# Rates of the DeltaNet heads: weights stationary in four column groups, then a sum by token

## The chip, the cores and the metric

One NeuronCore of a Trainium2 chip runs the whole program. The metric is the device time of one execution in microseconds (us); the median over several executions stands for a kernel.

## The reference, cut to what matters

The kernel is one inference step of a decoder trunk of two layers for 256 prompt tokens and 32 sample tokens (8 sequences of 4), 288 in all, with 1024 channels. Each layer projects its normed input `h` onto about 3000 columns. Eight of these columns are the rates of the four DeltaNet heads: a write strength `beta` and a decay `g` per head and token. Everything is float32.

```python
proj = h @ w_in[layer]
qkv_in, z, b_raw, a_raw, glu_u, glu_g = jnp.split(proj, [o1, o2, o3, o4, o5], axis=-1)
beta = jax.nn.sigmoid(b_raw)                               # (tokens, 4)
g = -jnp.exp(a_log) * jax.nn.softplus(a_raw + dt_bias)     # (tokens, 4)
o_a, s = gated_delta_rule(q, k, v, g, beta, s0)            # chunks of tokens, state carried
```

`b_raw` and `a_raw` together are `h` (288 x 1024) times an array of 1024 x 8. That product is what the change touches. Layer 1 ends in a router that multiplies `h` with another array of 1024 x 8.

## The kernel before

Channels lie on partitions: a tensor of 1024 channels is eight tiles (k = 0 to 7) of 128 partitions by T = 288 tokens. The normed input is kept three times: `hf` in float32 and `h_hi`, `h_lo`, its rounded part and the rest. Weights arrive as units of 1 MB in six buffers `raw`, in one order that is written out by hand (`SEQUENCE`). The queue of SyncE (SP) issues the load of unit u once unit u - 6 is used up. Some units are split by ScalarE (ACT, `split_hi`) and VectorE (DVE, `split_lo`, tile `wlo`) into `whi` and `wlo` before TensorE (PE) uses them; one such tile is 24 matmuls (L1669 to L1671). A tile from an unsplit unit is eight matmuls (L2014), each of two records in the trace, as are all plain float32 matmuls here.

The stage around the change is `project_in`, once per layer, twelve steps i = 0 to 11 of two tiles each. Steps 0 to 3 make the Conformer half, 4 to 9 the q, k and v tiles, 10 and 11 the output gate. Every engine has its own program with its own loop over i, and semaphores tie them together:

- PE: both tiles of a step (`project_tile`), then `token_rates` after i = 2, `decay_sums` after i = 5, then `ada_columns` and `ada_pair`. The last two make the modulation vectors: `ada_pair` (L1680) holds the conditioning vectors `cstat` stationary, 32 columns per k, writes tile k to partitions 32k to 32k + 31, and streams 512 weight columns; `ada_columns` (L1690) sums the four groups with a constant `comb` while it turns rows into columns. In layer 0 the pairs run after i = 1 to 8 with the columns one step later, in layer 1 the pairs from i = 2. A pair uses two units, and their buffers are what the next loads wait for.
- ACT: row copies (L681) for the pairs, the sigmoid of the Conformer gate (L761) at i = 0 to 3, `token_gates` at i = 4 (beta and half of the softplus), the exponentials of the decays at i = 6, copies of the q, k, v tiles, and `split_hi` two steps ahead.
- DVE: `fill` runs a fixed number of Conformer taps per step (`TAPS_IN`, L1108), `copy_rates` and `decay_steps` at i = 3, `decay_rates` at i = 4, `copy_decays` at i = 6, `conv_pair` from i = 5 (L1128), `modulation` at i = 10 (L1058, L1061), and `split_lo` two steps ahead.

`token_rates` multiplies with the tokens stationary: for three blocks of tokens (128, 128 and 32) and eight k, `hf` is the stationary operand and the eight weight columns stream (L1991). That is 24 matmuls per layer into 24 columns of PSUM bank 4, one group of eight per block. `decay_sums` later writes to columns 32 to 55 of the same bank. PE's `sums_qk` (L1805), after i = 9, waits for the `modulation` of i = 10.

The router of layer 1 (L2099) is already written the other way, with its weights stationary in four column groups, a copy, and a sum by token (L2114).

Of the kernel before, what the change touches and what calls it, by code (L numbers as in the profile page):

```python
# [34 lines left out]
P = 128  # L35
D = 1024
KD = D // P
# [140 lines left out]
for _l in range(DEPTH):  # L178
# [9 lines left out]
CCOL, NCONST = columns(  # L188
    [("ones", P), ("comb", NC_), ("eps6", 1), ("eps5", 1), ("epsq", 1), ("one", 1), ("ident", P), ("tri", P), ("after", P), ("m1l", P), ("m1t", P)]
    + [(f"mt{s}", P) for s in LEVELS] + [("outA", P), ("outQ", P), ("outAS", TS), ("outQS", TS)]  # L190
    + [("before", P), ("iota", P), ("triS", P), ("afterS", P), ("seqp", NB),
       ("ipart", 1), ("valid", 1),
       ("rank", 3 * NE), ("eye8", NE + 1)])

# [3 lines left out]
def constants():  # L198

    c = np.zeros((P, NCONST), np.float32)  # L200

    def put(name, a):
        lo, _ = CCOL[name]
        c[:a.shape[0], lo:lo + a.shape[1]] = a

    i, j = np.arange(P)[:, None], np.arange(P)[None, :]
    put("ones", np.ones((P, P)))
    put("ident", i == j)
    put("tri", i <= j)
    put("after", i > j)  # L210
    low = lambda s: (i // (2 * s) == j // (2 * s)) & (i % (2 * s) >= s) & (j % (2 * s) < s)
    put("m1l", low(1))
    put("m1t", low(1).T)
    for s in LEVELS:
        put(f"mt{s}", low(s).T)
    put("outA", np.where(i > j, -FAR, FAR))
    put("outQ", np.where(i <= j, FAR, -FAR))
    put("before", i < j)
    put("iota", np.broadcast_to(j, (P, P)))
    same = (i // TD == j // TD) & (i < TS) & (j < TS)  # L220
    put("triS", same & (i <= j))
    put("afterS", same & (i > j))
    put("outAS", np.where(same & (i > j), -FAR, FAR)[:TS, :TS])
    put("outQS", np.where(same & (i <= j), FAR, -FAR)[:TS, :TS])
    put("seqp", np.arange(P)[:, None] % TS // TD == np.arange(NB)[None, :])
    put("comb", np.concatenate([np.eye(P // 4, NC_)] * 4) * (i % (P // 4) < NC_))
    put("eps6", np.full((P, 1), 1e-6))
    put("eps5", np.full((P, 1), 1e-5))
    put("epsq", np.full((P, 1), P * 1e-6))
    put("one", np.ones((P, 1)))  # L230
    put("ipart", i)
    put("valid", i < TS)
    put("rank", np.broadcast_to(NE - np.tile(np.arange(NE), 3)[None, :], (P, 3 * NE)))
    put("eye8", np.eye(NE))
    return c
# [19 lines left out]
def program(nc, units, x_in, c_in, par_in, const_in, gdn_in, qst_in, cst_in,  # L255
            y_out, gdnp_out, gdns_out, qst_out, cst_out):
    ctx = ExitStack()
    with ctx:
# [165 lines left out]
        router_ready, parts_done, parts_copied = sem("router_ready"), sem("parts_done"), sem("parts_copied")  # L424
        moe_added = sem("moe_added")
        conv_first, conv_step = sem("conv_first"), sem("conv_step")
        qsq_ready, qss_ready, qrs_ready, qn_ready = sem("qsq_ready"), sem("qss_ready"), sem("qrs_ready"), sem("qn_ready")
        cmean_done, cent_ready, csq_ready, css_ready = sem("cmean_done"), sem("cent_ready"), sem("csq_ready"), sem("css_ready")
        crs_ready, cn_ready, cy_ready = sem("crs_ready"), sem("cn_ready"), sem("cy_ready")
# [226 lines left out]
        def _(act):  # L656
# [66 lines left out]
            def project_in(l):  # L723
                round_h(2 * l)
                for i in range(LEAD):
                    if i in SPLIT_IN[l]:
                        split_hi(in_split(l, i))
                for i in range(N_IN):
                    if i - 1 in ADA_BEHIND[l]:
                        row_copy(*ADA_BEHIND[l][i - 1], 1, 5 + (i - 1) % 2)  # L730
                    if i == 4:
                        token_gates(l)
                    if i == 6:
                        act.wait_ge(cum_ready, l + 1)
                        act.activation(eg, ps[:, 4, 32:56], ACT.Exp).then_inc(eg_ready, 1)
                    if I_QKV + 2 <= i < I_QKV + 2 + N_CONV - 1:
                        silu_tile(l, 2 * (i - I_QKV - 2))
                        silu_tile(l, 2 * (i - I_QKV - 2) + 1)
# [294 lines left out]
        def _(dve):  # L1033
# [105 lines left out]
            def project_in(l):  # L1139
# [4 lines left out]
                for i in range(N_IN):  # L1144
# [4 lines left out]
                        modulation(l, 1)  # L1149
                    if I_QKV < i <= I_QKV + N_CONV:  # L1150
                        conv_pair(l, i - I_QKV - 1)
                    if i == 3:
                        copy_rates(l)
                        decay_steps(l)
                    fill(l, TAPS_IN[l][i])
                    if i in SUMS_IN:
                        sample_taps(l, SUMS_IN[i])
                    if i in CONF_UNITS:
# [24 lines left out]
            def copy_rates(l):  # L1183

                step(dve.memset(ab, 0.0))
                dve.wait_ge(ab_done, l + 1)
                dve.tensor_copy(ab[:, 0:16], ps[:, 4, 0:16])
                dve.tensor_copy(ab[0:TS, 16:24], ps[0:TS, 4, 16:24]).then_inc(ab_copied, 1)

            def decay_steps(l):  # L1190

# [16 lines left out]
            def copy_decays(l):  # L1208

                dve.wait_ge(eg_ready, l + 1)  # L1210
                dve.wait_ge(beta_ready, l + 1)
                dve.tensor_copy(gcs, ps[:, 4, 32:44])
                dve.tensor_tensor(bEG, beta, eg[:, 0:12], ALU.mult).then_inc(beg_ready, 1)
                dve.wait_ge(beg_ready, l + 1)

# [221 lines left out]
            dve.wait_ge(par_loaded, 16)  # L1437
            modulation(0, 0)
            norm(0)
            dve.wait_ge(masks_loaded, 16)  # L1440
            project_in(0)
            mixer(0)
# [214 lines left out]
        def _(pe):  # L1657
# [326 lines left out]
            def token_rates(l):  # L1984

                pe.wait_ge(hf_ready, 4 * l + 2)
                a, _ = PCOL[f"wab{l}"]
                for b in range(3):
                    n = TS if b == 2 else P
                    for k in range(KD):  # L1990
                        last = mm(ps[0:n, 4, 8 * b:8 * b + 8], hf3[:, k, b * P:b * P + n], par[:, a + 8 * k:a + 8 * k + 8],  # L1991
                                  start=(k == 0), stop=(k == KD - 1))
                last.then_inc(ab_done, 1)

            def project_tile(l, i, s):
# [21 lines left out]
            def project_in(l):  # L2017

                for i in range(N_IN):
                    project_tile(l, i, 0)  # L2020
                    if i == N_IN - 1:
                        for b in range(2):
                            transpose_a(l, b, b, P)
                    project_tile(l, i, 1)
                    if i == 0:
                        pe.wait_ge(mod_ready, 1 + 2 * l)
                        pe.wait_ge(rstd_ready, 1 + 2 * l)
                    if i == 2:
                        token_rates(l)
                    if i == 5:  # L2030
                        decay_sums(l)
                    if i - 1 in ADA_BEHIND[l]:
                        ada_columns(*ADA_BEHIND[l][i - 1], 1)
                    if i in ADA_BEHIND[l]:
                        ada_pair(*ADA_BEHIND[l][i], 5 + i % 2)
                    if i == I_QKV + 5:
                        sums_qk(l)
                    if i == N_IN - 2:
                        pe.wait_ge(qrs_ready, 5 * l + 4)
                        for b in range(2):  # L2040
                            row_decays(l, b, b, P)
                        pe.wait_ge(qn_ready, 5 * l + 4)
                        for b in range(2):
                            pe.wait_ge(bank_free[b], uses_at[l][b])
                            block_products(l, b, b, P)

            def decay_sums(l):

                pe.wait_ge(g_ready, l + 1)
                for mask, maskS, c in (("tri", "triS", 32), ("after", "afterS", 44)):  # L2050

                    mm(ps[:, 4, c:c + 8], cc(mask), gg[:, 0:8], start=True, stop=True)
                    last = mm(ps[:, 4, c + 8:c + 12], cc(maskS), gg[:, 8:12], start=True, stop=True)
# [299 lines left out]
```

## Time and profile before

| | us |
|---|---|
| median of 3 runs | 1787.5 |
| lowest, highest | 1779.77, 1791.13 |
| span of the profiled execution | 1782.5 |
| PE busy in it | 1735.4 (97%) |
| DVE busy | 1370.1 (77%) |
| ACT busy | 1034.4 (58%) |

The profile is of one execution, whose span goes from the first to the last instruction. All durations below are from it. Busy shares are means over very different stages, so what an edit is worth has to be read in its own stage. The two projection stages stand at about 36 to 162 us (layer 0) and 514 to 633 us (layer 1).

### The profile page before, as it was taken

The numbers are of one execution on the slowest core, as the hardware profiler recorded it, in microseconds if no ns is written. First come the engines' busy times: TensorE is split into PE (matmuls) and PEld (weight loads), VectorE is DVE, ScalarE is ACT, GpSimd is POOL, SyncE is SP. The second block draws the span as 40 slices with busy tenths as digits, with TensorE's granted clock in tenths as the row PEclk, the third lists the DMA queues.
The fourth block names the chain that finished last, engine by engine and source line by source line (L and its number), as shares of the span: only waits on it lengthen the run. The fifth ranks groups of instructions, "written<-read, shape, count | busy, mean of one in ns | idle before, by whom it ended". The sixth has DMA issues, their size and how long they took to land.

```text
span 1782.5 us, 25547 instructions
## 1 busy us (share of the span) xinstructions
PE 1735.4 (97%) x9512; PEld 1452.5 (81%) x9512; DVE 1370.1 (77%) x1622; ACT 1034.4 (58%) x989; POOL 77.6 (4%) x97
## 2 busy tenths in 40 slices
PE   6999999999999999799999999999999999999997
PEld 3888967999978798578888888888888888888886
DVE  2698464454348974778898898898888988988998
ACT  3345423443333543167777777776777777767775
POOL 0112100000011130100000000000000000000000
PEclk9999998999999998899999999999999999999999
DMA  9785047444466510379999999999999999989997
GB/s 384 290 317 201 2 154 302 165 165 164 166 280 267 207 45 7 142 268 344 351 356 347 359 345 352 346 371 337 365 356 345 364 343 352 369 337 356 352 365 271
DMA packets 70187, 499.49 MB, mean 280 GB/s; under 512 B 7969, under 2 KB 8097, under 8 KB 11073
## 3 DMA queue, kind: packets, MB, share of 16 engines
q1 hardware_dynamic: 66528, 481.16, 71.2%
q0 software_dynamic: 3552, 16.87, 2.5%
q8 instruction: 72, 1.18, 0.3%
q14 instruction: 35, 0.28, 0.0%
HBM read 485.95 MB, written 12.05 MB: 279 GB/s over the span
## 4 chain that ended last, share of the span: by engine, by line
PE 91%; DVE 5%; DMA 2%; issue 1%; ACT 0%; SPq 0%; DVEq 0%
PE ps L2210 17%; PE ps L2212 17%; PE ps L2211 17%; PE ps L1669 5%; PE ps L1671 5%; PE ps L1670 5%; PE ps L2014 4%; PE ps L1851 3%; DMA raw<-units 2%; PE ps L1680 2%; PE ps L2155 1%; PE ps L2187 1%; DVE yc L1108 1%; PE ps L1760 1%; PE ps L1775 1%; PE ps L1773 1%
## 5 line engine op out<-in xcount | busy, mean ns | idle before, releaser
L1038 DVE TENSOR_TENSOR wlo<-raw,whi 128x2048 fp32r<-128x2048 f32 x384 | 876.7, 2292 | 191.3 <-ACT whi L664 191.3
L664 ACT ACTIVATE whi<-raw 128x2048 fp32r<-128x2048 f32 x384 | 735.7, 1918 | 267.9 <-PE ps L2212 213.2
L2210 PE MATMUL ps<-whi,ht_hi 128*128 128x512 f32 x896 | 356.3, 398 | 1.6 <-DVE ht_lo L1573 1.6
L2212 PE MATMUL ps<-whi,ht_lo 128*128 128x512 f32 x896 | 349.5, 390 | 0.0
L2211 PE MATMUL ps<-wlo,ht_hi 128*128 128x512 f32 x896 | 349.2, 390 | 0.0
L2210 PEld LDWEIGHTS ps<-whi,ht_hi 128*128 128x128 f32 x896 | 168.3, 188 | 37.4 <-issue 4.6
L2212 PEld LDWEIGHTS ps<-whi,ht_lo 128*128 128x128 f32 x896 | 168.1, 188 | 35.9
L2211 PEld LDWEIGHTS ps<-wlo,ht_hi 128*128 128x128 f32 x896 | 168.5, 188 | 31.6
L2210 PE MATMUL ps<-whi,at_hi 128*128 128x512 f32 x448 | 175.2, 391 | 0.0
L2212 PE MATMUL ps<-whi,at_lo 128*128 128x512 f32 x448 | 174.4, 389 | 0.0
L2211 PE MATMUL ps<-wlo,at_hi 128*128 128x512 f32 x448 | 174.4, 389 | 0.0
L1669 PE MATMUL ps<-h_hi,whi 128*128 128x288 f32 x560 | 168.8, 301 | 0.0
L1670 PE MATMUL ps<-h_lo,whi 128*128 128x288 f32 x560 | 166.5, 297 | 0.0
L1671 PE MATMUL ps<-h_hi,wlo 128*128 128x288 f32 x560 | 165.9, 296 | 0.0
L1669 PEld LDWEIGHTS ps<-h_hi,whi 128*128 128x128 f32 x560 | 106.3, 190 | 9.9 <-issue 9.8
L1671 PEld LDWEIGHTS ps<-h_hi,wlo 128*128 128x128 f32 x560 | 106.7, 191 | 0.0
L1670 PEld LDWEIGHTS ps<-h_lo,whi 128*128 128x128 f32 x560 | 106.5, 190 | 0.1
L1108 DVE SCALAR_TENSOR_TENSOR yc<-cpad,par,yc 128x256 f32<-128x256 f32 x240 | 103.8, 503 | 0.0
L2212 PEld LDWEIGHTS ps<-whi,at_lo 128*128 128x128 f32 x448 | 84.1, 188 | 17.6
L2211 PEld LDWEIGHTS ps<-wlo,at_hi 128*128 128x128 f32 x448 | 84.1, 188 | 16.7
L2210 PEld LDWEIGHTS ps<-whi,at_hi 128*128 128x128 f32 x448 | 84.1, 188 | 16.7
L2014 PE MATMUL ps<-hf,raw 128*128 128x288 f32 x352 | 91.0, 419 | 2.8 <-DVE hf L1088 2.8
(341 smaller groups left out, 2024.9 us busy)
## 6 DMA issues: line engine op xcount, KB each, us to landing
raw<-units SPq DMA_DIRECT2D x455, 1024.0 KB, 6.5
sst<-gdn_in POOLq DMA_DIRECT2D x8, 512.0 KB, 6.5
gdns_out<-sst POOLq DMA_DIRECT2D x8, 512.0 KB, 6.0
qst_out<-qpad POOLq DMA_DIRECT2D x2, 1890.0 KB, 8.8
cst_out<-cpad POOLq DMA_DIRECT2D x2, 1116.0 KB, 10.9
x<-x_in SPq DMA_DIRECT2D x1, 1152.0 KB, 9.0
y_out<-hf SPq DMA_DIRECT2D x2, 576.0 KB, 2.9
con<-const_in SPq DMA_DIRECT2D x1, 1141.5 KB, 18.7
```

What stands on the lines that cost most here:

```text
L664: act.activation(whi[s % NSPLIT][:, :], raw[u % NRAW][:, :], ACT.Copy).then_inc(hi_split, 1)
L1038: dve.tensor_tensor(wlo[s % NSPLIT][:, :], raw[unit_of(s) % NRAW][:, :], whi[s % NSPLIT][:, :].bitcast(F32), ALU.subtract).then_inc(lo_spl ...
L1108: dve.scalar_tensor_tensor(y, cp3[:, c, j:j + TP], w, y, ALU.mult, ALU.add).then_inc(tap_prompt, 1)
L1669: mm(out, w_hi, x_hi, start=start, stop=False)
L1670: mm(out, w_hi, x_lo, start=False, stop=False)
L1671: return mm(out, w_lo, x_hi, start=False, stop=stop)
L1680: last = mm(ps[32 * k:32 * k + 32, bank, :], cst3[:, 4 * half + k], raw[u % NRAW][:, k * 512:(k + 1) * 512], start=(half == 0), stop=(half ...
L1851: last = mm(ps[:, bank, 0:T], raw[u % NRAW][:, w], part, start=(k == 0), stop=(k == 3))
L2014: last = mm(ps[:, bank, 0:T], raw[u % NRAW][:, w], hf3[:, k], start=(k == 0), stop=(k == KD - 1))
L2210: mm(ps[:, bank, :], a_hi[:, a], whi[u % NSPLIT][:, w], start=(first and i == 0), stop=False)
L2211: mm(ps[:, bank, :], a_hi[:, a], wlo[u % NSPLIT][:, w], start=False, stop=False)
L2212: last = mm(ps[:, bank, :], a_lo[:, a], whi[u % NSPLIT][:, w], start=False, stop=(end and i == 3))
```

## The change

`token_rates` now holds the weights: for each k a stationary tile of 32 columns, of which eight columns (16 to 23 in layer 0, 24 to 31 in layer 1) are rate weights. It uses the spare columns of `cstat`, whose first nine hold the conditioning vectors. Four k go to four groups of 32 partitions of bank 4, and the other four are added to them: eight matmuls, 288 tokens streaming. ACT copies the 128x288 result to `ctmp` at the start of its i = 3. PE, between its two tiles of i = 3, multiplies that copy (tokens stationary, three blocks) with the new constant `pick`, which adds the four groups and picks the layer's eight rows: three matmuls. Results move to columns 288 to 311 of bank 4, and `decay_sums` to 320 to 343. DVE lays the rate weights of both layers into `cstat` once, after the first norm, and PE waits for that after i = 0. At i = 3 DVE now runs its taps ahead of `copy_rates` and `decay_steps`.

```diff
--- before.py
+++ after.py
@@ -188,7 +188,7 @@
 CCOL, NCONST = columns(
     [("ones", P), ("comb", NC_), ("eps6", 1), ("eps5", 1), ("epsq", 1), ("one", 1), ("ident", P), ("tri", P), ("after", P), ("m1l", P), ("m1t", P)]
     + [(f"mt{s}", P) for s in LEVELS] + [("outA", P), ("outQ", P), ("outAS", TS), ("outQS", TS)]
-    + [("before", P), ("iota", P), ("triS", P), ("afterS", P), ("seqp", NB),
+    + [("pick", 2 * 8), ("before", P), ("iota", P), ("triS", P), ("afterS", P), ("seqp", NB),
        ("ipart", 1), ("valid", 1),
        ("rank", 3 * NE), ("eye8", NE + 1)])
 
@@ -223,6 +223,7 @@
     put("outAS", np.where(same & (i > j), -FAR, FAR)[:TS, :TS])
     put("outQS", np.where(same & (i <= j), FAR, -FAR)[:TS, :TS])
     put("seqp", np.arange(P)[:, None] % TS // TD == np.arange(NB)[None, :])
+    put("pick", np.concatenate([np.eye(P // 4)[:, P // 4 - 2 * 8:]] * 4))
     put("comb", np.concatenate([np.eye(P // 4, NC_)] * 4) * (i % (P // 4) < NC_))
     put("eps6", np.full((P, 1), 1e-6))
     put("eps5", np.full((P, 1), 1e-5))
@@ -424,6 +425,7 @@
         router_ready, parts_done, parts_copied = sem("router_ready"), sem("parts_done"), sem("parts_copied")
         moe_added = sem("moe_added")
         conv_first, conv_step = sem("conv_first"), sem("conv_step")
+        rate_columns, rates_done, rates_copied = sem("rate_columns"), sem("rates_done"), sem("rates_copied")
         qsq_ready, qss_ready, qrs_ready, qn_ready = sem("qsq_ready"), sem("qss_ready"), sem("qrs_ready"), sem("qn_ready")
         cmean_done, cent_ready, csq_ready, css_ready = sem("cmean_done"), sem("cent_ready"), sem("csq_ready"), sem("css_ready")
         crs_ready, cn_ready, cy_ready = sem("crs_ready"), sem("cn_ready"), sem("cy_ready")
@@ -726,13 +728,16 @@
                     if i in SPLIT_IN[l]:
                         split_hi(in_split(l, i))
                 for i in range(N_IN):
+                    if i == 3:
+                        act.wait_ge(rates_done, l + 1)
+                        act.activation(ctmp[:, 0:T], ps[:, 4, 0:T], ACT.Copy).then_inc(rates_copied, 1)
                     if i - 1 in ADA_BEHIND[l]:
                         row_copy(*ADA_BEHIND[l][i - 1], 1, 5 + (i - 1) % 2)
                     if i == 4:
                         token_gates(l)
                     if i == 6:
                         act.wait_ge(cum_ready, l + 1)
-                        act.activation(eg, ps[:, 4, 32:56], ACT.Exp).then_inc(eg_ready, 1)
+                        act.activation(eg, ps[:, 4, 320:344], ACT.Exp).then_inc(eg_ready, 1)
                     if I_QKV + 2 <= i < I_QKV + 2 + N_CONV - 1:
                         silu_tile(l, 2 * (i - I_QKV - 2))
                         silu_tile(l, 2 * (i - I_QKV - 2) + 1)
@@ -1149,10 +1154,10 @@
                         modulation(l, 1)
                     if I_QKV < i <= I_QKV + N_CONV:
                         conv_pair(l, i - I_QKV - 1)
+                    fill(l, TAPS_IN[l][i])
                     if i == 3:
                         copy_rates(l)
                         decay_steps(l)
-                    fill(l, TAPS_IN[l][i])
                     if i in SUMS_IN:
                         sample_taps(l, SUMS_IN[i])
                     if i in CONF_UNITS:
@@ -1184,8 +1189,8 @@
 
                 step(dve.memset(ab, 0.0))
                 dve.wait_ge(ab_done, l + 1)
-                dve.tensor_copy(ab[:, 0:16], ps[:, 4, 0:16])
-                dve.tensor_copy(ab[0:TS, 16:24], ps[0:TS, 4, 16:24]).then_inc(ab_copied, 1)
+                dve.tensor_copy(ab[:, 0:16], ps[:, 4, T:T + 16])
+                dve.tensor_copy(ab[0:TS, 16:24], ps[0:TS, 4, T + 16:T + 24]).then_inc(ab_copied, 1)
 
             def decay_steps(l):
 
@@ -1209,7 +1214,7 @@
 
                 dve.wait_ge(eg_ready, l + 1)
                 dve.wait_ge(beta_ready, l + 1)
-                dve.tensor_copy(gcs, ps[:, 4, 32:44])
+                dve.tensor_copy(gcs, ps[:, 4, 320:332])
                 dve.tensor_tensor(bEG, beta, eg[:, 0:12], ALU.mult).then_inc(beg_ready, 1)
                 dve.wait_ge(beg_ready, l + 1)
 
@@ -1437,6 +1442,11 @@
             dve.wait_ge(par_loaded, 16)
             modulation(0, 0)
             norm(0)
+            dve.wait_ge(ada_used, 2 * len(ADA_HEAD))
+            for l in range(DEPTH):
+                last = dve.tensor_copy(cstat[:, :].rearrange("p (k c) -> p k c", k=KD)[:, :, 16 + 8 * l:24 + 8 * l],
+                                       pc(f"wab{l}").rearrange("p (k c) -> p k c", k=KD))
+            last.then_inc(rate_columns, 1)
             dve.wait_ge(masks_loaded, 16)
             project_in(0)
             mixer(0)
@@ -1984,12 +1994,20 @@
             def token_rates(l):
 
                 pe.wait_ge(hf_ready, 4 * l + 2)
-                a, _ = PCOL[f"wab{l}"]
+                cst3 = cstat[:, :].rearrange("p (k c) -> p k c", k=KD)
+                for half in range(2):
+                    for j in range(4):
+                        last = mm(ps[32 * j:32 * j + 32, 4, 0:T], cst3[:, 4 * half + j], hf3[:, 4 * half + j],
+                                  start=(half == 0), stop=(half == 1))
+                last.then_inc(rates_done, 1)
+
+            def rates_by_token(l):
+
+                pe.wait_ge(rates_copied, l + 1)
                 for b in range(3):
                     n = TS if b == 2 else P
-                    for k in range(KD):
-                        last = mm(ps[0:n, 4, 8 * b:8 * b + 8], hf3[:, k, b * P:b * P + n], par[:, a + 8 * k:a + 8 * k + 8],
-                                  start=(k == 0), stop=(k == KD - 1))
+                    last = mm(ps[0:n, 4, T + 8 * b:T + 8 * b + 8], ctmp[:, b * P:b * P + n], cc("pick")[:, 8 * l:8 * l + 8],
+                              start=True, stop=True)
                 last.then_inc(ab_done, 1)
 
             def project_tile(l, i, s):
@@ -2021,10 +2039,13 @@
                     if i == N_IN - 1:
                         for b in range(2):
                             transpose_a(l, b, b, P)
+                    if i == 3:
+                        rates_by_token(l)
                     project_tile(l, i, 1)
                     if i == 0:
                         pe.wait_ge(mod_ready, 1 + 2 * l)
                         pe.wait_ge(rstd_ready, 1 + 2 * l)
+                        pe.wait_ge(rate_columns, 1)
                     if i == 2:
                         token_rates(l)
                     if i == 5:
@@ -2047,7 +2068,7 @@
             def decay_sums(l):
 
                 pe.wait_ge(g_ready, l + 1)
-                for mask, maskS, c in (("tri", "triS", 32), ("after", "afterS", 44)):
+                for mask, maskS, c in (("tri", "triS", 320), ("after", "afterS", 332)):
 
                     mm(ps[:, 4, c:c + 8], cc(mask), gg[:, 0:8], start=True, stop=True)
                     last = mm(ps[:, 4, c + 8:c + 12], cc(maskS), gg[:, 8:12], start=True, stop=True)
```

## Rows read from the trace of the kernel before

**Rows 1.** The page: its first line, and the chain that ended last by engine.
```profile
span 1782.5 us, 25547 instructions
...
PE 91%; DVE 5%; DMA 2%; issue 1%; ACT 0%; SPq 0%; DVEq 0%
```

**Rows 2.** Chain of work, layer 0's input projection: start us, us, what.
```profile
60.68 4.88 PE ps L1991 x48
65.56 1.81 PE ps L1690 x8
67.37 3.34 PE ps L1680 x16
70.71 0.33 PE ps L1669
...
77.30 0.79 PE ps L1690 x8
78.09 1.85 PE ps L1680 x16
...
80.66 0.14 PE ps L1670
```

**Rows 3.** Windows, layer 0: busy of PE, PEld, DVE, ACT, POOL, clock, DMA, GB/s.
```profile
62.00:63.40 1.40, 1.40 (x15) 1.40 (x14) 1.40 (x5) 0.00 (x0) 0.00 (x0) 1.00 0.75 316
...
65.50:67.30 1.80, 1.80 (x11) 1.77 (x9) 1.80 (x6) 1.59 (x1) 0.00 (x0) 0.50 0.00 0
...
95.80:99.30 3.50, 3.50 (x32) 2.04 (x31) 3.50 (x10) 1.34 (x4) 0.00 (x0) 1.00 0.60 253
```

**Rows 4.** Chain of work, layer 1's input projection.
```profile
535.24 4.92 PE ps L1991 x47
540.16 3.51 PE ps L1680 x14
```

**Rows 5.** Windows, layer 1, behind the pair of matmuls.
```profile
543.70:545.00 1.30, 1.30 (x6) 1.30 (x7) 1.30 (x1) 0.60 (x1) 0.00 (x0) 0.58 0.80 334
```

**Rows 6.** Waits of PE, layer 1: waiter, releaser, us in total, times, longest.
```profile
PE ps L1805 <- DVE gain L1061: 2.4, 1, 2.4
```

**Rows 7.** Timeline of DVE, layer 1: start, us, instruction [idle before].
```profile
551.34 0.42 DVE L1163 TENSOR_TENSOR cpad<-ps,sg 128x256 f32<-128x256 f32 x1 [0.48 <-ACT sg L761]
...
554.14 2.29 DVE L1038 TENSOR_TENSOR wlo<-raw,whi 128x2048 fp32r<-128x2048 f32 x1 [2.27 <-ACT whi L664]
...
565.39 2.29 DVE L1038 TENSOR_TENSOR wlo<-raw,whi 128x2048 fp32r<-128x2048 f32 x1 [2.13 <-ACT whi L664]
```

**Rows 8.** Timeline of ACT, layer 0.
```profile
60.72 0.41 ACT L761 ACTIVATE sg<-ps 128x288 f32<-128x288 f32 x1 [3.44 <-PE ps L1671]
...
65.18 1.91 ACT L664 ACTIVATE whi<-raw 128x2048 fp32r<-128x2048 f32 x1 [4.05 <-DMA raw<-units]
```

**Rows 9.** Timeline of DVE, layer 0.
```profile
40.88 2.29 DVE L1038 TENSOR_TENSOR wlo<-raw,whi 128x2048 fp32r<-128x2048 f32 x1 [0.51 <-ACT whi L664]
...
71.56 0.17 DVE L1187 COPY small<-ps 128x16 f32<-128x16 f32 x1
```

**Rows 10.** Waits of DVE, 60 to 112 us.
```profile
DVE wlo L1038 <- ACT whi L664: 5.0, 2, 3.5
DVE cpad L1163 <- ACT sg L761: 0.9, 1, 0.9
```

**Rows 11.** Chain of work, the router.
```profile
745.58 1.19 PE ps L2099 x8
```

**Rows 12.** Windows, the router.
```profile
745.50:746.80 1.30, 1.22 (x9) 0.30 (x10) 0.17 (x3) 0.00 (x0) 1.21 (x2) 0.50 0.00 0
```

**Rows 13.** Chain of work, the mixer's state products, layer 0 and layer 1.
```profile
215.24 3.47 PE ps L1793 x32
...
685.90 4.47 PE ps L1793 x32
```

## The prediction

> **What bounds the kernel now.** I read the page first. Its span is 1782.5 us and its chain of work that ended last is TensorE (PE) for 91% of the span [rows 1]; so what PE is given to do, in order, sets the time unless another engine is late. The change touches one stage of each layer, the input projection, so I read the chain there, then the granted clock in windows, and last the waits and timelines of VectorE (DVE) and ScalarE (ACT), to see who would be late if PE were faster.
>
> In layer 0 the 24 matmuls of `token_rates` (L1991, two records each) stand on the chain for 4.88 us [rows 2]. The reader is to see what comes right behind them too: the `ada_columns` matmuls (L1690) take 1.81 us and the `ada_pair` matmuls (L1680) 3.34 us, while the same two pieces one step later take 0.79 and 1.85 us [rows 2]. The windows say why: the granted clock is 1.00 (2.4 GHz) at 62.0, and 0.50 (1.2 GHz) at 65.5, behind some 3 us of streams of only 8 columns, during which PE was busy without a break; no load of weights was under way by then either (DMA share 0.00) [rows 3]. In layer 1 the same: 4.92 us of L1991, then a pair of 3.51 us [rows 4], and 1.3 us more of the next tile at a mean clock of 0.58 [rows 5]. So the narrow matmuls cost their own time and the slow clock behind them.
>
> **The change part by part.**
>
> *Removed.* Layer 0: 4.88 us of L1991. If the clock stays up, also 1.81 - 0.79 = 1.02 and 3.34 - 1.85 = 1.49 us [rows 2]. Together 7.39. Layer 1: 4.92; the pair 3.51 - 1.85 = 1.66 [rows 2, 4]; of the 1.3 us at 0.58, 0.42 x 1.3 = 0.55 [rows 5]. Together 7.13.
>
> *Added on PE: eight matmuls of 32 stationary columns with 288 tokens streaming, in four column groups.* The nearest row is `ada_pair`, the same form with 512 columns: 16 records in 1.85 us at full clock [rows 2]; 288/512 of it is 1.04 us. From above the router in layer 1 bounds it, which is this very form: four matmuls (8 records) in 1.19 us [rows 11] at a clock of 0.50 [rows 12], so 2.38 us for eight. I take 1.04, since the projection runs at full clock.
>
> *Added on PE: three matmuls per layer that sum the groups by token* (8 columns stream, the tokens are stationary, six records). They have the form of L1991, 4.88/48 = 0.10 us a record [rows 2], so 0.61 us; at half clock, by L1690's 1.81/8 = 0.23 a record [rows 2], 1.36 us. I take 0.61.
>
> *Changes between whole array and column groups.* The first matmul behind a pair takes 0.33 us on the chain, another of such a tile 0.14 [rows 2]: a return from groups costs 0.2 us. In layer 0 `ada_columns` stands between the new groups and the pair's, so there is one change more: 0.2 us. In layer 1 no columns stand there, and I add nothing. The Trainium skill (TensorEngine Tiling (Array Packing), Tiling Modes, Key Properties) speaks against the change here: every change of tiling mode drains TensorE. It gives no price; the trace agrees, with 0.2 us, and the rule's sum is no other than the row's.
>
> *The new wait of PE on ACT.* Between the two tiles of i = 3 PE waits for ACT's copy of the 128x288 rates. An ACT pass over a bank of 128x288 takes 0.41 us [rows 8]. In layer 0 the copy is queued behind `split_hi`, which waits for a load until 65.18 and takes 1.91 [rows 8]: the copy is done at 67.5. PE, from 60.68: 1.04 + 0.79 + 0.2 + 1.85 and a tile of 3.3 (half of 70.71 to 77.30, [rows 2]) = 67.9. It doesn't wait, by 0.4 us. In layer 1 the `split_hi` ahead of the copy waited for no load, so the slack is wider. Behind PE's wait stand tile (3,1) and the next pair, and behind these the loads, since a pair frees two buffers; if the cover is gone, each microsecond is lost one for one. ACT itself gains 0.41 us of work; it idled 4.05 us before that `split_hi` [rows 8].
>
> *Moved on DVE.* The 8 taps of i = 3 go ahead of `copy_rates` and `decay_steps`. Nothing is added there. The gates come 3.2 us later in DVE's order, but ACT wants them only at i = 4 and PE (`decay_sums`) after i = 5; worth nothing. *Added on DVE*: two copies that lay the rate columns into `cstat`, about 0.2 us each (a small copy is 0.17 [rows 9]), where DVE idled 0.51 us before its first `wlo` [rows 9]: nothing. With that cover gone they'd cost 0.4. The table of constants grows by 16 columns, which its load hides.
>
> *What is late next.* Layer 0: PE comes 7.39 - 1.04 - 0.61 - 0.2 = 5.5 us earlier. Loads are issued when a pair frees buffers, and the loads stood still while PE was slow [rows 3], so they shift with PE. DVE follows too: it idled 5.0 us for ACT and 0.9 for the sigmoid between 60 and 112 [rows 10], and PE never waited for DVE later in this stage. Gain 5.5 us. Layer 1: PE comes 7.13 - 1.65 = 5.5 us earlier, but here PE does wait for DVE later, 2.4 us at L1805 for the `modulation` of i = 10 [rows 6]. DVE has the same work between, and only its idle time can give: 0.48 + 2.27 + 2.13 = 4.88 us [rows 7]. All three are waits for things that PE's earlier arrival pulls forward. So layer 1 gains 4.9 us, and PE waits 0.6 us more at L1805. Downstream all waits are relative, so the gain reaches the end.
>
> **Sum.** 5.5 + 4.9 = 10.4 us. Against the profiled execution: 1782.5 - 10.4 = 1772.1 of span, and the runs lie about 5 us above that span. Against the median: 1787.5 - 10.4 = 1777.1 us.
>
> **The rivals.**
>
> *A, the clock stays low.* For it: the three matmuls by token still stream 8 columns. Against it: sums, `ada_columns` and a pair in a row, 3.5 us, ran at 1.00 [rows 3], and the new sequence in layer 0 (1.04 + 0.79 + 1.85) is its like. If the slow stretch stays as it is and the new matmuls run at full clock, the layers gain 4.88 - 1.85 = 3.0 and 4.92 - 1.65 = 3.3 us: 1781.2. If they run at half clock too, 4.88 - 2.38 - 1.36 - 0.2 = 0.9 and 1.2: 1785.4. The Trainium skill (TensorE: Matmul & The Clock Gate, Part 1) ties the fall of the clock to idle stretches of TensorE; by that rule the narrow streams would not be its cause, the fall would stay, and the result would be 1781.2. The trace disagrees: PE was busy 1.40 of 1.40 us ahead of the fall, in both layers behind the same matmuls [rows 3, 4].
>
> *B, DVE keeps layer 1.* If one of the three idles is a load that comes by bandwidth and not by its issue, or ACT's extra wait holds `split_hi` back, layer 1 gives next to nothing: 1787.5 - 5.5 = 1782.0. For it: after 565 DVE didn't wait for anything until PE waited for it [rows 6, 7]. Against it: it was PE's slowness that held the loads back, in layer 0 down to a DMA share of 0.00 [rows 3].
>
> *C, clocks elsewhere fall otherwise.* The same 32 small matmuls of the mixer took 3.47 us in layer 0 and 4.47 in layer 1 [rows 13], where the clock fell on their way. A shift in time can add or take such a fall, some 2.5 us by what the one in layer 0's projection costs (1.02 + 1.49): 1774.6 or 1779.6 with the gain intact. This is part of the forecast's own range.
>
> *D, the other side.* PE waits at the new wait for ACT, since the load ahead of `split_hi` lands late. It loses from a landing of 65.6 on; the gain is eaten up when it lands at 65.2 + 0.4 + 10.4 = 76.0, and at 78 the time is 1789.5, slower than before. Nothing in the trace shows a load that late.
>
> *E, the change doesn't do what it says: the groups run one after another.* Then the eight matmuls take 4 x 1.04 = 4.2 us, 3.1 more in each layer; these gain 5.5 - 3.1 = 2.4 us each: 1782.7. Against it: `ada_pair` is written in the same way, and the router's four matmuls took 1.19 us at half clock [rows 11, 12], no more than 1.19/2 = 0.6 at full clock.
>
> **How the numbers follow.** Forecast 0.67 (C inside it), A 0.15, B 0.12, D 0.03, E 0.03. The likeliest is 1777.1 and is what I predict. Its own range is 2.5 us of C and about 5 us for how the runs shown scatter (1779.8 to 1791.1, so their median is good to a few microseconds): 1769 to 1784. A and B lie at 1781 to 1785; the range that leaves 2 in 10 out is 1769 to 1786. One per cent is 17.9 us and about what a measurement of this kernel can tell from no change. Faster by over 1% (under 1769.6) needs the forecast, a fall of C less and a fast median: 0.08. Slower by over 1% (over 1805) is D at its worst or luck: 0.03. The rest, 0.89, is within 1%.
>
> **What would show it.** In the profile after: the line of the new groups at about 1.0 us a layer and the by-token line at 0.6; the pair behind them at 1.85 and a granted clock of 1.00 there (else A); no wait of PE on ACT at the by-token matmuls (else D); DVE's idle time between i = 3 and i = 6 nearly gone in layer 1 and PE's wait at L1805's place near 3 us; from the start of `token_rates` to that place 5 us less. I'm wrong if the clock falls anyway, if DVE doesn't move up, or if falls elsewhere weigh more than the 10 us.

## The result

The changed kernel takes 1802.32 us (median of 7 runs, 1792.72 to 1805.12), the kernel before 1784.38 us (7 runs, 1779.62 to 1791.13). The ratio on record is 1.0076 with a 95% interval of 1.0055 to 1.0097 (it is not the quotient of the two medians, which is 1.0101): slower by about 1%, where 10 us less were forecast, and outside the range that was given (1769 to 1786). The ratios below leave out two slow executions, one of 2183 us of the kernel with the narrow matmuls in parts and one of 3484 us of the kernel with the old order on DVE.

The page after, its first line and the chain that ended last by engine (before: [rows 1]):

```profile
span 1796.0 us, 25448 instructions
...
PE 90%; DVE 7%; DMA 2%; issue 1%; ACT 0%; SPq 0%; DVEq 0%
```

The rows of the chain of layer 0 that answer to [rows 2]: L2000 is the eight matmuls in column groups, L1700 `ada_columns`, L1690 `ada_pair`, L1679 the first matmul of a split tile, L2009 the sum by token.

```profile
59.82 1.11 PE ps L2000 x16
60.93 0.99 PE ps L1700 x8
61.92 1.85 PE ps L1690 x16
63.77 0.33 PE ps L1679
...
67.15 0.50 PE ps L2009 x6
```

Where 4.88 + 1.81 + 3.34 us stood, there are now 1.11 + 0.99 + 1.85, and 0.50 for the sum by token. The windows over this stretch (columns: busy time and count of PE, PE's weight loads, DVE, ACT, GpSimd, then granted clock, DMA share, GB/s) have the clock at 1.00 all through, where [rows 3] has 0.50:

```profile
59.00:68.00 9.00, 9.00 (x80) 6.65 (x79) 9.00 (x25) 3.11 (x4) 0.00 (x0) 1.00 0.79 302
60.93:63.80 2.87, 2.87 (x25) 1.41 (x25) 2.87 (x8) 0.69 (x1) 0.00 (x0) 1.00 0.36 151
```

In layer 1 the same: behind the column groups the pair takes 1.83 us instead of 3.5, and the clock over both is 1.00.

```profile
532.10:535.30 3.20, 3.20 (x36) 1.31 (x36) 3.20 (x9) 2.75 (x4) 0.00 (x0) 1.00 0.25 33
```

So in this stage PE did what the prediction said. The chain at the router, and the waits of PE between 500 and 740 us (answering to [rows 11] and [rows 6]):

```profile
737.26 1.19 PE ps L2120 x8
```

```profile
PE ps L1815 <- DVE gain L1066: 4.5, 1, 4.5
```

At the router the changed kernel is 745.58 - 737.26 = 8.3 us ahead, of 10.4 forecast. It ends 1796.0 - 1782.5 = 13.5 us behind. All that is lost, 21.8 us, is lost behind the router, 21.6 of it in the expert stage, which no line of the change touches. One group of matmuls there (`wlo` streams, the tokens `ht_hi` are stationary), before and after; the line gives count, busy us, mean ns of one:

```profile
L2211 PE MATMUL ps<-wlo,ht_hi 128*128 128x512 f32 x896 | 349.2, 390 | 0.0
```

```profile
L2232 PE MATMUL ps<-wlo,ht_hi 128*128 128x512 f32 x896 | 353.5, 395 | 0.0
```

The same 896 matmuls take 395 ns instead of 390. These are latencies of pipelined matmuls. From start to start, by the trace's records, two of them stand 227.6 ns apart before and 233.2 ns after. The windows say the same by count, in 990 us of experts at a granted clock of 1.00 in both: PE gets through 4555 matmuls before and 4457 after.

```profile
770.00:1760.00 990.00, 990.00 (x4555) 818.05 (x4554) 876.85 (x604) 718.02 (x489) 0.00 (x0) 1.00 0.93 352
```

```profile
770.00:1760.00 990.00, 990.00 (x4457) 801.32 (x4456) 863.41 (x594) 701.40 (x477) 0.00 (x0) 1.00 0.92 346
```

The expert stage, from its first hidden matmul to its last, takes 996.1 us before and 1017.7 us after. It has 8 experts x 42 units x 12 = 4032 such matmuls. 4032 x 5.6 ns = 22.6 us, close to the 21.6 us that the stage grew by. DMA moves the data of both at a share of 0.92 to 0.93, and the trace has no wait of PE for another engine in these 990 us. So PE's own rhythm is slower, by 2.5% from start to start, at full clock.

### The profile page after: what moved, and what is told of

It reads as the page before. It is cut to its first block, busy times and chain, and to the rows that moved or that the text cites. A ratio compares the mean times of both kernels' runs of the same rounds, so it can differ in the third digit from the quotient of the medians.

```text
span 1796.0 us, 25448 instructions
## 1 busy us (share of the span) xinstructions
PE 1745.3 (97%) x9460; PEld 1442.0 (80%) x9460; DVE 1376.4 (77%) x1624; ACT 1034.2 (58%) x991; POOL 82.6 (5%) x97
## 4 chain that ended last, share of the span: by engine, by line
PE 90%; DVE 7%; DMA 2%; issue 1%; ACT 0%; SPq 0%; DVEq 0%
PE ps L2231 18%; PE ps L2233 17%; PE ps L2232 17%; PE ps L1679 5%; PE ps L1680 5%; PE ps L1681 5%; PE ps L2032 4%; PE ps L1861 3%; DVE yc L1113 2%; DMA raw<-units 2%; PE ps L1690 2%; PE ps L2208 1%; PE ps L2176 1%; PE ps L1770 1%; PE ps L1785 1%; PE ps L1783 1%
## 5 line engine op out<-in xcount | busy, mean ns | idle before, releaser
L2231 PE MATMUL ps<-whi,ht_hi 128*128 128x512 f32 x896 | 360.0, 402 | 1.7 <-DVE ht_lo L1583 1.7
L2233 PE MATMUL ps<-whi,ht_lo 128*128 128x512 f32 x896 | 353.7, 395 | 0.0
L2232 PE MATMUL ps<-wlo,ht_hi 128*128 128x512 f32 x896 | 353.5, 395 | 0.0
L1679 PE MATMUL ps<-h_hi,whi 128*128 128x288 f32 x560 | 167.2, 299 | 0.0
L1679 PEld LDWEIGHTS ps<-h_hi,whi 128*128 128x128 f32 x560 | 106.4, 190 | 8.5 <-issue 8.4
```

The lines of the kernel that those rows point to most:

```text
L1679: mm(out, w_hi, x_hi, start=start, stop=False)
L2231: mm(ps[:, bank, :], a_hi[:, a], whi[u % NSPLIT][:, w], start=(first and i == 0), stop=False)
L2232: mm(ps[:, bank, :], a_hi[:, a], wlo[u % NSPLIT][:, w], start=False, stop=False)
L2233: last = mm(ps[:, bank, :], a_lo[:, a], whi[u % NSPLIT][:, w], start=False, stop=(end and i == 3))
```

## The experiments

Three theories of that loss:

- **place**: the new constant `pick` is 16 columns, 64 bytes per partition. It stands in the table of constants, and every tile allocated behind the table moves by 64 bytes. Among these are all operands that the experts hold stationary (`ht_hi`, `ht_lo`, `at_hi`, `at_lo`), but not the weights that stream (`whi`, `wlo`), which are allocated ahead of it.
- **program**: PE's instruction stream is another one, and that alone changes its rhythm.
- **rates**: the matmuls in column groups leave PE in another state.

### The place alone, on the kernel before

```diff
         con = keep("con", NCONST)
+        keep("pad", 16)
```

> The kernel before, with 64 unused bytes per partition behind the table of constants and nothing else changed, so that all tiles allocated behind it lie where they lie in the changed kernel. Theory place (the moved addresses slow the experts' matmuls): the second hidden group of the experts goes from a mean of 390 to 395 ns, the experts take some 22 us more, the projections gain nothing, and the time is about 1.012 of before (1806 us). Theory program (the other instruction stream of PE does it) or theory rates (the new matmuls leave something behind): 390 ns and a ratio of 1.000.

Measured: 1806.14 us, ratio 1.0124 (1.0086 to 1.0162), spacing 233.2 ns, experts 1017.7 us. The page's group:

```profile
L2212 PE MATMUL ps<-wlo,ht_hi 128*128 128x512 f32 x896 | 353.5, 395 | 0.0
```

64 unused bytes, with no other change, cost 21 us, and they give the experts of the changed kernel to a tenth of a microsecond. Theory place is shown; rates is not needed. One point of the expectation missed: the projections did gain. Their 288-column matmuls stand 132.2 ns apart instead of 133.3, and this trace reaches the router 2.5 us sooner than that of before (743.10 instead of 745.58), with the clock at 0.50 for the same 51.2 us on the way.

### 32 bytes

The same edit with `keep("pad", 8)`.

> The kernel before with 32 unused bytes behind the constants. Theory place: a spacing other than 390 ns, I expect 395 or more since the tiles then start off both 64 and 128 bytes; experts 20 us or more longer. Theories program and rates: as before.

Measured in one execution: 1808.66 us, spacing 233.1 to 233.3 ns, experts 1017.2 us. It agrees with theory place.

### Another instruction stream at the old place

```diff
+            pe.wait_ge(con_loaded, 16)
+            pe.wait_ge(par_loaded, 16)
             project_in(0)
```

> The kernel before with two more waits in PE's program, both long met, and all addresses as before. Theory place: 390 ns in the experts and no change of time. Theory program: the spacing of the experts' matmuls changes, towards 395 ns and up to 20 us more.

Measured in one execution: 1795.44 us, but a spacing of 227.6 ns and experts of 996.1 us. The group is that of the kernel before:

```profile
L2213 PE MATMUL ps<-wlo,ht_hi 128*128 128x512 f32 x896 | 349.2, 390 | 0.0
```

Theory program falls: in the experts nothing changed. All 11 us that this execution lies above the profiled one of before come ahead of the router, which it reaches at 753.5 instead of 742.5 us (start of the matmuls by the records), and the clock goes with them: between 30 us and the router the trace's clock records have it at 0.50 for 75.1 us, in the trace of before for 51.2 us. One of these falls, over the first two tiles of layer 1, is not there before (the same two tiles ran at 1.00):

```profile
515.00:525.20 10.20, 10.20 (x35) 7.12 (x32) 4.92 (x3) 5.89 (x5) 0.00 (x0) 0.50 1.01 422
```

The kernel before itself ran from 1779.82 to 1793.78 us beside it, so I take the falls for scatter, not for an effect of two waits; it was run once, and that is not shown. It tells how little a single time, or a lead read from one trace, is worth below 10 us here.

### 64 bytes more on the changed kernel

```diff
         con = keep("con", NCONST)
+        keep("pad", 16)
```

> The changed kernel with 64 more unused bytes behind the constants, so that the tiles behind them move by 128 bytes in all against before. Theory place, if a step of 128 bytes brings the fast spacing back: 390 ns, the 8 us lead at the router reaches the end, ratio to before 0.994 to 0.996 (1774 to 1777 us). Theory program or theory rates: still 395 ns and a ratio near 1.008.

Measured: 1797.51 us, ratio 1.0068 (1.0044 to 1.0092), spacing 233.0 ns, experts 1016.2 us. A step of 128 bytes in all does not bring the fast spacing back in the experts. It does so in the projections, whose 288-column matmuls stand 133.3 ns apart before, 132.2 after the change and 133.3 here. So the period of the effect is not 128 bytes, or not for all forms of matmul. Left open after this: a larger period, or what the addresses are compared with.

### A map of addresses, PE alone

Behind the last result of the kernel before, PE runs 24 matmuls of the experts' form for each of 72 pairs of operand addresses, with nobody else at work.

```diff
+            pe.wait_ge(y_ready, 2)
+            for n, (o, m) in enumerate(PAIRS):
+                for k in range(24):
+                    i = k % 3
+                    mm(ps[:, n % 8, :], ht_hi[1][:, o + 128 * i:o + 128 * i + 128],
+                       whi[0][:, m + 512 * i:m + 512 * i + 512], start=(k == 0), stop=(k == 23))
```

> The kernel before, and behind its last result 1728 matmuls of PE alone, 24 for each of 72 pairs of operand addresses (the stationary and the moving operand each shifted in steps of 64 bytes over 512, and the stationary in steps of 32). It adds about 400 us by design. Theory place: the spacing from start to start depends on the difference of the two addresses modulo 512 and takes the values 227 ns and 233 ns seen in the experts. Rival (the slow spacing comes from other engines' reads or from loads): with PE alone all pairs run equally, below 227 ns.

The window over it (ACT, DVE and GpSimd at 0.00, clock 1.00):

```profile
1780.00:2178.00 398.00, 398.00 (x1725) 323.94 (x1725) 0.00 (x0) 0.00 (x0) 0.00 (x0) 1.00 0.01 3
```

Mean time from start to start in ns, without the first six of each pair. Rows: the stationary operand's address modulo 512; columns: the moving operand's. (The labels take the start of the program's memory to be 128 modulo 512, which no trace shows; what is read from them needs only the differences.)

```
        0     64    128    192    256    320    384    448
  0  226.6  228.9  232.0  233.5  226.6  228.9  232.1  233.5
 64  233.5  226.7  228.9  232.0  233.5  226.7  228.9  232.0
128  232.0  233.5  226.6  228.9  232.0  233.5  226.6  228.9
192  228.8  232.0  233.5  226.6  228.9  232.1  233.5  226.7
256  226.6  228.9  232.0  233.5  226.7  228.9  232.0  233.5
320  233.5  226.7  228.9  232.0  233.5  226.6  228.9  232.0
384  232.8  233.3  226.9  228.8  232.8  233.3  227.9  228.7
448  228.7  232.0  233.5  226.7  228.7  232.0  233.5  226.6
```

The diagonals say it (row 384 is up to 1.3 ns off them): what counts is the stationary address less the moving one, modulo 256. At 0 a matmul takes 226.6 ns, at 192 bytes 228.9, at 128 bytes 232.0 and at 64 bytes 233.5. Differences of 32, 96, 160 and 224 bytes, tried at one moving address, gave 233.2 to 234.3. No other engine is needed for it. The kernel before has 0 for all its experts' matmuls: by its layout the tiles of the expert stage begin 86272 = 337 x 256 bytes behind `whi`, and their slices lie at multiples of 256 from there. The changed kernel has 64, the one with 32 bytes 32, and the one with 64 bytes more 128. The rival fell, and so did my modulo 512: half of it is enough. Why PE's rhythm follows this difference, no run here shows.

### The changed kernel with its tiles 512 bytes from their old places

```diff
         con = keep("con", NCONST)
+        keep("pad", 112)
```

> The changed kernel with 448 unused bytes behind the constants: with the 64 of the new constant that is 512 bytes against before, so every tile behind them has the address of before modulo 512, the distance between the slices that a matmul holds stationary. Theory place, modulo 512: the experts' matmuls go back to 390 ns and 227 ns from start to start, the experts to 996 us, the lead at the router reaches the end, ratio 0.994 (0.992 to 0.997). Rival, place in another form (an absolute address or what overlaps it): 395 ns, ratio 1.007.

Measured: 1779.08 us (12 runs), ratio 0.9972 (0.9957 to 0.9987), spacing 227.7 ns in the first (`ht`) and 227.1 ns in the second (`at`) product of the experts, experts 996.3 us. Spacing and stage are as expected; the ratio lies just above its range.

```profile
span 1774.4 us, 25448 instructions
...
L2233 PE MATMUL ps<-wlo,ht_hi 128*128 128x512 f32 x896 | 349.3, 390 | 0.0
```

With the place repaired the change is a gain: the profiled execution is 8.1 us below that of before, and the ratio of the runs gives 0.28%, about 5 us.

### The experts' tiles alone

Only the tiles of the expert stage get a new base, `r1 = r0 + 192`, on the changed kernel: 256 bytes from their old places. All others keep their 64.

```diff
+        r1 = r0 + 192
-        ht_hi = [at(f"ht_hi{i}", r0 + 70656 * i, D, F32R) for i in range(2)]
+        ht_hi = [at(f"ht_hi{i}", r1 + 70656 * i, D, F32R) for i in range(2)]
...
```

The other 13 names of that stage follow in the same way.

> The changed kernel as it is, but with the tiles of the expert stage alone moved by 192 bytes more, so that they stand 256 bytes behind their places of before while all other tiles keep their 64. Theory place, by the address map (the spacing depends on the stationary operand's address less the moving one's, modulo 256, and is least at 0): the experts' matmuls at 227 ns from start to start and 996 us in all, the projections' 288-column matmuls at 132.2 as in the changed kernel (133.3 before), so some 2 us less than the variant with 448 bytes: ratio 0.995 to 0.997. Rival (it takes all tiles, or a distance of 512): experts at 233 ns, ratio 1.007.

Measured: 1780.86 us, ratio 0.9957 (0.9938 to 0.9977). The experts stand 227.7 and 227.1 ns apart and take 996.3 us; the projections' matmuls keep their 132.2 ns. Both as expected. Against the variant before this one the intervals overlap, so these times can't show the 2 us of the projections.

### Does the clock fall because of the unbroken narrow matmuls?

The kernel before, with its 24 narrow matmuls per layer in three parts of eight, with tiles of the projection between the parts.

```diff
+                    if i == 2:
+                        token_rates(l, 0)
                     project_tile(l, i, 1)
-                    if i == 2:
-                        token_rates(l)
+                    if i in (1, 2):
+                        token_rates(l, i)
```

> The kernel before with its 24 narrow matmuls per layer in three parts, between wide tiles: the block of 32 tokens after i = 1, the first of 128 between the two tiles of i = 2 and wait of none, the second not run (a third of the rates is left out, so its output is not the reference's). My reading of the clock (the unbroken narrow streams make it fall): the granted clock stays at 1.00 there, the pair behind takes 1.85 us, and the two layers gain 2.5 + 2.2 us and the left-out third 3.3 us: 0.995 to 0.997 of before. Rival (the fall has another cause): the pair still takes 3.3 to 3.5 us.

The text on record describes the kernel wrongly in one point: all three blocks are run, nothing is left out, and the 3.3 us for the left-out third don't count. By the theory 2.5 + 2.2 = 4.7 us remain, a ratio of 0.9974. Measured: 0.9976 (0.9953 to 0.9999); but the medians hardly differ (1783.0 and 1783.6 us), so it is the trace that decides here, and not the time. Chain of layer 0, the first part and the pair behind it, then the second part:

```profile
51.10 1.68 PE ps L1991 x16
52.79 1.85 PE ps L1680 x16
...
58.03 1.69 PE ps L1991 x16
...
63.01 0.60 PE ps L1991 x16
```

```profile
51.00:56.00 5.00, 5.00 (x43) 3.54 (x42) 1.17 (x3) 1.56 (x2) 0.00 (x0) 1.00 0.56 180
60.00:72.00 12.00, 12.00 (x105) 10.35 (x104) 11.91 (x30) 2.92 (x3) 0.00 (x0) 1.00 0.69 242
```

The narrow matmuls take 1.68 + 1.69 + 0.60 = 3.97 us instead of 4.88 (before, the clock fell within them, at 63.5 us by the trace's records), the clock stays at 1.00 and the pair takes 1.85 us. In layer 1 the same (1.00 from 525 to 545 us). So the reading holds: it was the unbroken stretch of 8-column streams. It doesn't rest on one trace alone. In the traces of all five kernels that keep the 24 narrow matmuls in one piece the clock falls to 0.50 during them or right behind, in both layers; in none of the seven others does it fall at this place. The Trainium skill (TensorE: Matmul & The Clock Gate, Part 1) ties the fall to idle stretches; this case shows a fall with PE busy throughout and none when the same matmuls are broken up.

### The order on DVE

The changed kernel with the 448 bytes, and the taps of i = 3 behind `copy_rates` again.

```diff
-                    fill(l, TAPS_IN[l][i])
...
+                    fill(l, TAPS_IN[l][i])
```

> The changed kernel with 448 unused bytes, and DVE's taps of i = 3 behind copy_rates and decay_steps again, as before the change. Prediction's step (the move is worth nothing): ratio 0.997, as the same kernel with the new order, within 0.001. Rival (the new order is what lets DVE keep up, since copy_rates would wait for PE's sum by token): DVE waits at copy_rates and PE's wait at sums_qk in layer 1 grows beyond 4.2 us.

Measured: 1779.11 us, ratio 0.9954 (0.9939 to 0.9969), against 0.9972 for the new order. That is 0.0018 apart where 0.001 was expected, but the intervals overlap. DVE has no wait at `copy_rates`, and PE's wait for the modulation in layer 1 is 4.3 us instead of 4.2. The move is worth nothing that shows, as predicted.

### Why layer 1 gave less: GpSimd beside DVE

In layer 1 the prediction let DVE give 4.88 us of idle time. DVE gave it up, but the lead grew by less. Timeline of DVE and of GpSimd in the kernel with the 448 bytes, then of both in the kernel before:

```profile
548.05 2.62 DVE L1044 TENSOR_TENSOR wlo<-raw,whi 128x2048 fp32r<-128x2048 f32 x1
550.60 7.67 DVE L1114 SCALAR_TENSOR_TENSOR yc<-cpad,par,yc 128x256 f32<-128x256 f32 x16
```

```profile
547.85 4.99 POOL L619 TENSOR_TENSOR taps_s<-cpad,par 128x248 f32<-128x248 f32 x4 [22.67 <-DVE yc L1121]
```

```profile
556.35 6.42 DVE L1108 SCALAR_TENSOR_TENSOR yc<-cpad,par,yc 128x256 f32<-128x256 f32 x16
```

```profile
551.00 2.58 POOL L616 TENSOR_TENSOR taps_s<-cpad,par 128x248 f32<-128x248 f32 x4 [22.66 <-DVE yc L1115]
```

Before, GpSimd's four products of sample taps (2.58 us) ran mostly while DVE waited for its split, in the idle 2.27 us of [rows 7]. Now DVE has no idle time there, the products run beside its split and its 16 taps, and both sides take longer: 4.99 instead of 2.58 us, 2.62 instead of 2.29, and 7.67 instead of 6.42. I took three of the four products away:

```diff
-                    for t in range(TD):
+                    for t in range(1 if c == 1 else TD):
```

> The changed kernel with 448 unused bytes, and GpSimd makes only one of four products of its second group of sample taps in each layer (three quarters of that group's products are left out, so the sample outputs are not the reference's). Theory contention (in layer 1 GpSimd's group now runs beside DVE's taps of i = 4 instead of in DVE's idle time): the 16 taps go from 7.7 to about 6.6 us, the split ahead from 2.6 to 2.4, and PE's wait for the modulation in layer 1 from 4.2 to about 3.0. Rival (DVE is late for another reason): taps stay at 7.7 and the wait at 4.2.

```profile
555.07 6.42 DVE L1114 SCALAR_TENSOR_TENSOR yc<-cpad,par,yc 128x256 f32<-128x256 f32 x16
```

```profile
PE ps L1816 <- DVE gain L1067: 3.0, 1, 3.0
```

The 16 taps are back at 6.42 us and PE waits 3.0 us instead of 4.2. The split ahead of the taps, beside which the one product left still ran, stays at 2.63 us, where 2.4 were expected. So of the shortfall in layer 1 about 1.2 us is this overlap. The kernel with the narrow matmuls in parts shows the same overlap: there too DVE's idle time shrinks, the products take 4.86 us and the taps 7.27. The wait alone would not show it, since it is 2.4, 3.4 and 4.0 us in three traces of kernels whose taps take 6.42 us (before, with 64 unused bytes, with two more waits).

## Why the prediction was wrong

Point by point, by its own steps.

- **Removed, both layers: right.** L1991's 4.88 us, and with it the slow clock behind it. A clock of 1.00 and a pair of 1.85 us stand where the prediction wanted them.
- **Added on PE: right to 0.2 us.** Column groups 1.11 us (1.04 predicted), sum by token 0.50 (0.61), one change between array forms 0.2 (`ada_columns` takes 0.99 instead of 0.79 behind the groups). The sum lacks a second such 0.2 us: the first matmul of the tile behind the sum by token takes 0.33 us instead of 0.13. The Trainium skill's rule of the drain (TensorEngine Tiling (Array Packing), Tiling Modes, Key Properties) agrees with a price at a change of form. But the price is not that of the groups alone: with the narrow matmuls in parts, `ada_columns` takes 0.99 us behind the block with 32 stationary columns too, where no groups stand.
- **Wait of PE on ACT: right.** PE waits for nothing between 60 and 75 us. ACT's copy started at 64.93 behind its split and was done at 65.3, when PE came at 67.15. The slack was 1.8 us and not 0.4, since the load ahead of the split had landed 2.1 us sooner (the split starts at 63.11 instead of 65.18).
- **Layer 0: right.** From the start of the rates to the mixer the lead over the kernel before grows from 0.8 to 6.3 us: 5.5, as predicted.
- **Layer 1: right in mechanism, too large.** PE is 5.7 us further at the tile behind the pair (5.5 predicted), but DVE passes on less: 4.9 predicted; between the rates and the mixer the lead grows from 3.0 to 6.6 us, 3.6. The mis-sized term is "DVE has the same work between": I took its duration to stay when its idle time went, and GpSimd's overlap made the split and the taps 0.3 + 1.3 = 1.6 us longer. PE's wait at this place is 4.5 us instead of the 3 I expected.
- **"Downstream all waits are relative, so the gain reaches the end": only up to the router.** Falls of the clock elsewhere came at other places (rival C): layer 0's state products took 4.20 + 1.91 us instead of 3.47 + 1.20, the first two tiles of layer 1 (unsplit) 9.49 instead of 7.86, and a fall in layer 1's mixer [rows 13] was lighter. The clock records between 30 us and the router have 0.50 for 45.3 us after and 51.2 before. Of the 51.2 the two falls behind the rates were 13.6, so the others grew by 7.7 us. The lead at the router was 8.3 us.

```profile
196.58 4.20 PE ps L1803 x32
200.78 1.91 PE ps L1916 x8
```

```profile
202.75 3.47 PE ps L1793 x32
206.22 1.20 PE ps L1906 x8
```

- **"The table of constants grows by 16 columns, which its load hides": this is the step that failed.** I priced the growth as bytes to load, and put it at nothing. Its price is the place of everything allocated behind it, against the place of the tiles ahead of it: 21.6 us more in the experts and, by the spacing there, an estimate of 2200 x 1.1 ns = 2.4 us less in the split tiles of projections and dense layer. None of the rivals had it. The kernel before stood, for its longest stage, at the best difference there is (0), so by the map any growth that was no multiple of 256 bytes could only lose there.
- **The sum against the median.** I took the runs to lie 5 us above the profiled span, from a median of three. The profiled execution of the repaired kernel has a time 1.8 us above its span (1776.22 and 1774.4). My base of 1787.5 was 1 to 4 us high: four sets of 7 to 23 runs of before have medians of 1784.4, 1785.0, 1783.6 and 1786.6. That doesn't change the sign.

With the place repaired by 448 bytes, 0.9972 (0.9957 to 0.9987) is 2 to 8 us of gain, in the profiled executions 8.1, and the forecast of 10.4 lies above both. With the experts' tiles alone moved it is 0.9957 (0.9938 to 0.9977), 4 to 11 us, which holds the forecast. So the rest of the sum was about right or somewhat too large; GpSimd's overlap and moved falls of the clock are what is known of the difference. Not settled: which falls of the clock a shift in time brings or takes, since they differ from execution to execution.

## What to carry to other kernels

When an edit adds a tile or a constant, look at what is allocated behind it: the operands of a matmul-bound stage can change their distance, and 64 bytes made this kernel's longest stage 2.2% longer. Put new constants behind those operands, or pad to the next 256 bytes, and compare the start-to-start time of an untouched stage first whenever a result comes out on the wrong side. And an engine's idle time is only worth its length if nobody else was using it: ask which other engine ran meanwhile.

## What the runs showed of the hardware

- The time from start to start of 128x128 by 512-column fp32r matmuls at full clock depends on the stationary address less the moving one, modulo 256 bytes: 226.6 ns at 0, 228.9 at 192, 232.0 at 128, 233.5 at 64, and 233.2 to 234.3 at odd multiples of 32. It does so with all other engines idle.
- Both spacings are steady rhythms: 226, 227, 227 at a difference of 0; 231, 236 or 234, 233, 233 at 64. At the start of the map the fast one is found after seven matmuls (336, 231, 231, 236, 228, 233, 230, then 227).
- With 288 columns the effect is smaller and the map does not carry over: 133.3 ns where the difference steps between 0 and 128 bytes, 132.2 ns where it steps between 64 and 192 (by the map's means the second would be the slower), 134.2 to 134.4 ns with 32 bytes.
- TensorE's clock fell to 0.50 while PE was busy with 8-column streams (five traces, both layers), and did not when these were broken into parts with tiles between them (one trace, both layers).
- Time spent at 0.50 differs from execution to execution: 51.2 us between 30 us and the router in three traces (before, with 64 and with 32 unused bytes), 75.1 us in the one with two more waits.
- GpSimd's four products took 4.99 us beside DVE's two-input work and 2.58 us in DVE's idle time; DVE's 16 taps took 7.67 us against 6.42.
